# Two layers' attention passes: one unit's rounding moved behind the last two softmax copies, its low part moved between two results

## The reference, cut to what matters

```python
def _token_mixing(n, w_in, ..., br_nsa, br_dil, br_fox, w_out, cos, sin):
    proj = n @ w_in
    ...
    y_a = _nsa_attention(...)          # 4 heads, compressed, selected and window keys
    y_b = _dilated_attention(...)      # 6 heads in 3 patterns
    y_c = _forgetting_attention(...)   # 6 heads, causal, with forget gates
    g_a, g_b, g_c = jnp.split(jax.nn.sigmoid(merge_g), 3, axis=-1)
    merged = g_a * (y_a @ br_nsa) + g_b * (y_b @ br_dil) + g_c * (y_c @ br_fox)
    return merged @ w_out
```

## Time and profile before

| | |
|---|---|
| Median of 3 runs | 1996.29 us (1994.49 to 1996.79) |
| The profiled execution | 1996.17 us |
| Its span in the trace | 1994.4 us |
| PE busy | 1921.5 us, 96% |
| DVE busy | 1381.7 us, 69% |
| ACT busy | 990.9 us, 50% |
| Mean granted TensorE clock | 0.987 of full speed |
| Loads | 458.43 MB, 230 GB/s over the span |

### The profile page before, as it was taken

One profiled execution on the slowest core, in us unless ns is written; L12 is line 12 of the kernel. 1 busy time (PEld: TensorE's weight loads), 2 busy tenths in 40 slices (PEclk: granted clock), 3 DMA queues, 4 the chain that ended last, 5 costly groups with the idle time before them and its releaser, 6 DMA issues.

```text
span 1994.4 us, 30127 instructions
## 1 busy us (share of the span) xinstructions
PE 1921.5 (96%) x12742; PEld 1718.9 (86%) x12773; DVE 1381.7 (69%) x1475; ACT 990.9 (50%) x1153; POOL 92.5 (5%) x117
## 2 busy tenths in 40 slices
PE   7989999999999999999998999999999999999997
PEld 3977778888887999899997899989998999879997
DVE  4889668898897777776445787778776563475444
ACT  3356457777775433454554433343334544544432
POOL 0330100000001000000000000000002000000000
PEclk9989989999999999999999999999999999999999
DMA  9555549999994787574322487648774552135554
GB/s 370 197 226 200 192 163 350 348 375 346 349 373 186 292 301 285 190 274 158 140 85 106 191 337 287 262 175 338 293 278 162 190 190 85 64 127 186 180 184 159
DMA packets 63878, 458.43 MB, mean 230 GB/s; under 512 B 7040, under 2 KB 7296, under 8 KB 8832
## 3 DMA queue, kind: packets, MB, share of 16 engines
q1 hardware_dynamic: 63744, 456.51, 60.7%
HBM read 455.43 MB, written 1.05 MB: 229 GB/s over the span
## 4 chain that ended last, share of the span: by engine, by line
PE 59%; issue 23%; DVE 10%; ACT 4%; DMA 1%; DVEq 1%; POOL 1%; POOLq 0%; SPq 0%; ACTq 0%
PE PS L359 17%; PE PS L361 16%; PE PS L360 16%; DVE acc L332 3%; DVE wlo L286 3%; ACT whi L280 2%; PE PS L345 1%; PE PS L972 1%; DMA ada<-in_ada 1%; PE PS L1339 1%; PE PS L1265 1%; PE PS L1351 1%; PE PS L2100 1%; PE PS L2125 1%; POOL Z L491 0%
## 5 line engine op out<-in xcount | busy, mean ns | idle before, releaser
L286 DVE TENSOR_TENSOR wlo<-raw,whi 128x2048 fp32r<-128x2048 f32 x282 | 646.2, 2294 | 324.2 <-ACT whi L280 318.9
L280 ACT ACTIVATE whi<-raw 128x2048 fp32r<-128x2048 f32 x282 | 538.4, 1912 | 349.5 <-PE PS L361 304.3
L359 PE MATMUL PS<-whi,hhi 128*128 128x256 f32 (+1 forms) x1568 | 503.1, 321 | 15.3 <-DVE wlo L286 7.1
L361 PE MATMUL PS<-whi,hlo 128*128 128x256 f32 (+1 forms) x1568 | 491.4, 313 | 0.0
L360 PE MATMUL PS<-wlo,hhi 128*128 128x256 f32 (+1 forms) x1568 | 491.2, 313 | 0.0
L359 PEld LDWEIGHTS PS<-whi,hhi 128*128 128x128 f32 x1568 | 302.7, 193 | 41.0 <-issue 11.1
L359 PE MATMUL PS<-hhi,whi 128*128 128x256 f32 x1152 | 327.0, 284 | 2.7 <-DVE mod L354 2.7
L361 PE MATMUL PS<-hhi,wlo 128*128 128x256 f32 x1152 | 326.0, 283 | 0.0
L360 PE MATMUL PS<-hlo,whi 128*128 128x256 f32 x1152 | 326.0, 283 | 0.0
L361 PEld LDWEIGHTS PS<-whi,hlo 128*128 128x128 f32 x1568 | 302.2, 193 | 16.9
L360 PEld LDWEIGHTS PS<-wlo,hhi 128*128 128x128 f32 x1568 | 302.7, 193 | 15.4
(11 more groups left out here) (412 smaller groups left out, 1813.3 us busy)
## 6 DMA issues: line engine op xcount, KB each, us to landing
raw<-in_stream SPq DMA_DIRECT2D x285, 1024.0 KB, 4.9
ada<-in_ada SPq DMA_DIRECT2D x92, 1024.0 KB, 4.8
ada<-in_stream SPq DMA_DIRECT2D x48, 1024.0 KB, 5.0
raw<-in_ada SPq DMA_DIRECT2D x3, 1024.0 KB, 15.9
xs<-in_x SPq DMA_DIRECT2D x1, 1024.0 KB, 12.0
Z<-in_ada SPq DMA_DIRECT2D x1, 1024.0 KB, 19.9
Z<-in_ctx SPq DMA_DIRECT2D x1, 1024.0 KB, 12.1
masks<-in_masks SPq DMA_DIRECT2D x2, 512.0 KB, 9.9
```

The source lines that it names most:

```text
L280: nc.scalar.activation(whi[:, s], src, ACT.Copy).then_inc(hi_ready, 1)
L286: nc.vector.tensor_tensor(wlo[:, s], src, whi[:, s].bitcast(F32), ALU.subtract).then_inc(lo_ready, 1)
L359: nc.tensor.matmul(out_, ah, bh, start=start, stop=False, skip_group_check=check)
L361: return nc.tensor.matmul(out_, al, bh, start=False, stop=stop, skip_group_check=check)
```

## The change

For gate unit 10 alone, the rounding leaves step 17. ACT now rounds BR0+1 in step 19, after the copy of pass 18 and ahead of the copy of pass 19. DVE takes its low part between `fox_out(14, ...)` and `fox_out(18, ...)`. No instruction is added, removed or changed in shape; PE, POOL and SP keep their order.

```diff
@@ act_layer, the loop over the passes
                     nc.scalar.activation(pt2[:, p % 2, 0:384], PS[:, 2 + p % 2, 0:384], ACT.Copy).then_inc(*B["pt2_out"].up)
-                if done[1]:
+                if done[1] and done[0] < 10:
                     conv_hi(act, CG[done[0]] + RING, E0)
+                if i == PASSES2 - 1:
+                    conv_hi(act, CG[10] + RING, E0)
@@ dve_layer, behind the loop
             fox_out(14, 4, 4, 0)
+            conv_lo(dve, CG[10] + RING, E0)
             fox_out(18, 2, 5, 0)
```

## The result

| | before | after |
|---|---|---|
| Median of the first runs | 1996.16 us (4 runs) | 1980.16 us (4 runs, 1979.84 to 1983.81) |
| Profiled execution, span | 1996.17, 1994.4 | 1980.08, 1978.3 |
| Ratio, 95% interval | | 0.9925 (0.9908 to 0.9942) |
| Median of later runs | 1993.5 (62 more runs, 1989.4 to 1999.2) | 1981.0 (22 in all, 1977.4 to 1985.0) |

The bottom row puts the difference at 12.5 us. Its 62 runs of the kernel before were taken on four chips, with medians of 1992.7, 1995.7, 1994.1 and 1994.6.

A forecast was written before the change was run, and what follows sets the result against it. TensorE, busy 96% of the span, was taken as the bound, with an 8.0 us wait for ACT's exponential. Savings of 5.85 and 5.83 us, moves at zero cost, gave 1996.17 - 11.7 = 1984.5 us, own range 1983 to 1986.5, widened to 1981.8 to 1988.2.

The forecast's parts named there:

- The wait: TensorE's wait ahead of pass 18's transposes, once per layer, would go: 4.16 us saved in the first layer.
- copy 17: ACT's copy of pass 17 was to start at 1045.24 and end by 1045.7, just ahead of product 17.
- the maxima: DVE's row maxima were to follow their scores directly: that of pass 18 ending at 1043.13, of 19 at 1045.60.
- the start of the gate tile: On TensorE, the first tile of gate unit 11 was to start at 1046.59 and take 2.96 us.
- The covers: TensorE's work was to hide both moved steps, with 1.4 us to spare on ACT and 0.7 us on DVE.
- the late load: Load of WO0+1, issued at about 1051.1 instead of 1047.40, was to land with 10.8 us left and cost zero.
- the free time of DVE behind the second gate tile: An overrun of DVE's low part would first eat unit 11's second gate tile, leaving about 3 us more free.
- The clock term: Gate tile behind the wait was to run at full clock: 1.69 us saved between transposes 18 and 19, first layer.
- the clock isn't given back: Rival: the waits go but the gate tile stays slow; 8.3 us saved, 1987.9 us; chance 0.07.
- the sum's starting point: The savings were taken from the profiled 1996.17 us, as it lay 0.1 us from the median of three runs.
- the clock shifts elsewhere: Rival: half clock at the feed-forward start is lost or gained, 1.7 us a place; 1982.8 or 1986.2; chance 0.09.
- more than 10: TensorE was to want BR0+1 only after BR0, more than 10 us after BR0+1 is ready at 1051.1.

The follow-up runs named there:

- warm: Kernel before, nothing moved, with 17 matmuls on zeros put into TensorE's wait ahead of the transposes of pass 18: 1988.67 us, ratio 0.9975.
- before_filled: Kernel before, order unchanged, with matmuls on zeros in TensorE's wait ahead of pass 18's transposes and in four other idle places: 1988.34 us, ratio 0.9972.

## Why the prediction was wrong

- **The wait.** 4.16 us a layer forecast, 5.10 - 0.94 = 4.16 measured in both. The offsets taken from rows held to 0.1 us: copy 17, the maxima, the start of the gate tile.
- **The covers.** 1.4 and 0.7 us forecast, 1.33 and 0.68 found; the late load cost nothing. Doubling each step confirmed the slack, also the free time of DVE behind the second gate tile, though not quite all of it: 0.35 us was lost where I had none.
- **The clock term**, 1.69 us a layer, was right for the one profile that it was read from and too small for the kernel: six of eight waits showed 2.8 to 3.0, and the mean over the eight is 2.6, so the sum for two layers lacked 1.9 us. Its rival (the clock isn't given back) was wrong outright; warm shows that idle time is the cause.
- **The step that failed is the sum's starting point**: "1996.17 - 11.7", with "no correction is due". The three runs and the profile all sat high. Over 62 later runs the kernel before has a median of 1993.5 (1992.7 to 1995.7 by chip), and that profile had 13.6 and 6.8 us at half clock in two places where its later profiles had 6.8 and 0. The rival *the clock shifts elsewhere* was the right mechanism, given 0.09 and 1.7 us a place, while one place alone (240 to 262 us) differed by 3.4 us in time between two profiles of the kernel before. It named the wrong place, too: the start of the feed-forward part had 3.4 us at half clock in the first profile of before and in that of after. It should have been part of the forecast's own range. 1993.5 less the 13.6 that the profiles give is 1979.9, less the 11.7 of my sum 1981.8; the median over 22 runs is 1981.0. That 1980.16 came as near as 1.6 us to the range, and that the gain was larger than forecast and not smaller, is luck: of the 16.1 us between the two profiled executions, 4.4 came from places that the sum held fixed.
- **Smaller slips.** BR0 is 24 matmuls, not the 48 given ahead of the prediction, so TensorE wants BR0+1 9.7 us behind its low part (1057.93 by 1048.20), not "more than 10"; it changed nothing. The chances of the cases that count as faster add up to 0.96, not 0.95.
- Shown: the wait, its chain through DVE, the clock behind it, the additivity of the layers. Not shown: what decides, in one and the same program, whether the clock falls behind a short pause, and whether the change makes it fall more often in the output product. The Trainium skill ("TensorE: Matmul & The Clock Gate", Part 1, the HAM clock gate) says that the gate's window is free-running and isn't reset when a kernel starts. That would fit a fall in one profile and none in the next, but no run tested it.

## What to carry to other kernels

In a chain that goes round several engines, look for the step with no filler work left behind it: the rounding of a unit, which TensorE never waited for between steps with gate tiles, cost 4 us of wait in the first step without one. The chain was held by the engine that waited in its order for something not urgent (DVE, 4.4 us for a rounding whose unit was needed 19 us after its low part), so move that wait first; moving its producer was worth under a tenth of the whole. Price a wait of TensorE at its length plus the slow matmuls behind it, take that from several profiles, and start a forecast from as many runs as can be had.

## What the runs showed of the hardware

One program's profiles differ by up to 3.4 us in time in a single place (240 to 262 us), with another granted clock. At the start of the second layer's passes the clock was 0.80 over 17 us in one profile of before and 1.00 over the same 17 us in the next, with the same pause of 1.10 us in front; 3.0 us in time. A pause of 4.0 us lost it in all eight cases, for 3.4 or 6.8 us of half clock. Matmuls on zeros kept it: the clock was 1.00 in and behind all four such waits that were filled (warm, before_filled).
